# A decoder trunk on one core: the weights' low parts move from GpSimd to VectorE

## The reference

```python
for l in range(DEPTH):
    h = rms_norm(x, mix_norm[l])
    z = h @ w_in[l]
    c_q, c_kv, k_r, hq, hf, hi, hg, guv, gates = split_sizes(z, IN_SIZES)
    y_a = mla(c_q, c_kv, k_r, ..., cos, sin) @ w_branch_a[l]
    y_b = hgrn2(hq, hf, hi, hg, lower_bounds[l], hg_head_norm[l]) @ w_branch_b[l]
    y_c = gmlp(guv, gm_ln_g[l], gm_ln_b[l], gm_w_s[l], gm_b_s[l]) @ w_branch_c[l]
    g_a, g_b, g_c = jnp.split(jax.nn.sigmoid(gates), 3, axis=-1)
    x = x + (g_a * y_a + g_b * y_b + g_c * y_c) @ w_mix_out[l]
    h = rms_norm(x, xa_norm[l])
    m = rms_norm(mem, mem_norm[l])
    x = x + cross_attn(h, m, xa_w_q[l], xa_w_kv[l], xa_w_o[l])
    h = rms_norm(x, ffn_norm[l])
    gt, up = jnp.split(h @ ffn_w_in[l], 2, axis=-1)
    x = x + (jax.nn.silu(gt) * up) @ ffn_w_out[l]
return rms_norm(x, final_norm)
```

## Time and profile before

| | |
|---|---|
| median of 3 runs | 2306.24 us |
| lowest, highest | 2301.65, 2307.18 us |
| span of the profiled execution, first to last instruction | 2302.0 us |
| time of that execution beside its span | not given apart; the median of the runs is 4.2 us above the span |
| granted TensorE clock, mean over the span | 0.990 |
| GpSimd: busy, instructions | 899.5 us, 418 |
| ScalarE: busy, instructions | 1001.0 us, 1455 |

### The profile page before, as it was taken

One profiled execution on the slowest core, in us unless ns is written; L12 is line 12 of the kernel. 1 busy time (PEld: TensorE's weight loads), 2 busy tenths in 40 slices (PEclk: granted clock), 3 DMA queues, 4 the chain that ended last, 5 costly groups with the idle time before them and its releaser, 6 DMA issues.

```text
span 2302.0 us, 31660 instructions
## 1 busy us (share of the span) xinstructions
PE 2206.0 (96%) x10429; PEld 1788.9 (78%) x10429; DVE 1252.5 (54%) x1695; ACT 1001.0 (43%) x1455; POOL 899.5 (39%) x418
## 2 busy tenths in 40 slices
PE   6999999999999999999999999999999999999998
PEld 5787777667877888888878877776687878888886
DVE  6757666665654544441267566765556446444312
ACT  5665545444444333232356655454453444332223
POOL 4332333234544344444443332222354434444442
PEclk8999999999999999999999999999999999999999
DMA  5222221223333333333342222122343323333331
GB/s 160 72 67 65 65 57 47 56 77 112 113 95 101 90 92 101 92 98 92 95 121 65 69 60 65 39 62 52 102 115 92 109 84 95 98 101 92 94 100 63
DMA packets 368096, 197.10 MB, mean 86 GB/s; under 512 B 24268, under 2 KB 361528, under 8 KB 367928
## 3 DMA queue, kind: packets, MB, share of 16 engines
q1 hardware_dynamic: 362008, 185.68, 28.9%
q10 hardware_dynamic: 5920, 9.31, 1.3%
HBM read 191.68 MB, written 2.10 MB: 84 GB/s over the span
## 4 chain that ended last, share of the span: by engine, by line
PE 80%; DVE 10%; issue 5%; ACT 3%; DMA 1%; ACTq 0%; DVEq 0%; POOL 0%; SPq 0%; POOLq 0%
PE PS L573 23%; PE PS L575 23%; PE PS L574 23%; PE PS L792 2%; PE PS L733 1%; PE PS L815 1%; DVE rstd L1532 1%; DVE xqL L1306 1%; DVE mp L1612 1%; DMA spare<-mq 1%; DVE dec L1496 1%; DVE sqs L1274 1%; PE PS L630 1%; PE PS L632 1%; PE PS L631 1%
## 5 line engine op out<-in xcount | busy, mean ns | idle before, releaser
L513 POOL TENSOR_TENSOR wL<-raw,wH 128x1024 fp32r<-128x1024 f32 (+4 forms) x406 | 890.3, 2195 | 1361.0 <-ACT wH L936 1360.5
L936 ACT ACTIVATE wH<-raw 128x1024 fp32r<-128x1024 f32 (+4 forms) x406 | 384.1, 947 | 982.2 <-PE PS L575 892.1
L573 PE MATMUL PS<-hH,wH 128*128 128x512 f32 x1696 | 675.2, 398 | 16.0 <-ACT wH L936 11.0
L575 PE MATMUL PS<-hH,wL 128*128 128x512 f32 x1696 | 663.0, 391 | 0.0
L574 PE MATMUL PS<-hL,wH 128*128 128x512 f32 x1696 | 663.0, 391 | 0.0
L573 PEld LDWEIGHTS PS<-hH,wH 128*128 128x128 f32 x1696 | 319.9, 189 | 87.7 <-issue 13.1
L574 PEld LDWEIGHTS PS<-hL,wH 128*128 128x128 f32 x1696 | 320.1, 189 | 68.3 <-issue 3.6
L575 PEld LDWEIGHTS PS<-hH,wL 128*128 128x128 f32 x1696 | 319.5, 188 | 68.3
L1284 DVE TENSOR_TENSOR xT<-xT,PS 128x512 f32<-128x512 f32 x48 | 33.0, 688 | 264.3 <-PE PS L575 264.3
L1301 DVE TENSOR_TENSOR fm<-PS,rh 128x512 f32<-128x512 f32 x44 | 30.4, 692 | 201.1 <-PE PS L575 201.1
L575 PE MATMUL PS<-fH,wL 128*128 128x512 f32 x352 | 136.9, 389 | 0.0
(11 more groups left out here) (340 smaller groups left out, 3427.9 us busy)
## 6 DMA issues: line engine op xcount, KB each, us to landing
raw<-in_w_in SPq DMA_DIRECT2D x106, 512.0 KB, 3.9
raw<-in_ffn_w_in SPq DMA_DIRECT2D x88, 512.0 KB, 3.8
raw<-in_xa_w_kv SPq DMA_DIRECT2D x32, 512.0 KB, 3.8
raw<-in_ffn_w_out SPq DMA_DIRECT2D x32, 512.0 KB, 3.9
raw<-in_w_mix_out SPq DMA_DIRECT2D x16, 512.0 KB, 4.0
raw<-in_xa_w_q SPq DMA_DIRECT2D x16, 512.0 KB, 3.9
raw<-in_xa_w_o SPq DMA_DIRECT2D x16, 512.0 KB, 4.0
raw<-in_ffn_w_out SPq DMA_DIRECT2D x16, 384.0 KB, 3.4
```

The costliest lines, as they stand in the source:

```text
L513: nc.gpsimd.tensor_tensor(wL[:, s, 0:w], raw[:, r, 0:w], wH[:, s, 0:w].bitcast(F32), ALU.subtract).then_inc(*did("gpsimd", "lo", n))
L573: nc.tensor.matmul(o, w0, xh(k0 + k), start=(first and k == 0), stop=False)
L575: ins = nc.tensor.matmul(o, w1, xh(k0 + k), start=False, stop=(last and k == kts - 1))
L936: nc.scalar.activation(wH[:, PLACE[n] % NS, 0:w], raw[:, PLACE[n] % NR, 0:w], ACT.Copy).then_inc(*did("scalar", "hi", n))
```

## The change

The loop over the units leaves GpSimd. VectorE makes the same subtractions: those of units 0 to 3 at the head of the layer's loop, and that of each unit in freed(n) at the end of its step for unit n, after that step's evictions and low parts. What counts a "lo" is now VectorE's semaphore, for which SyncE and TensorE wait.

```diff
@@ GpSimd
             layers("gpsimd")
-            with pool.Fori(0, L) as l:
-                for n, (name, j) in enumerate(UNITS):
-                    kt, m = shape_of(name, j)
-                    w = kt * m
-
-                    pool.wait_ge(*after(l, "hi", n))
-                    s, r = PLACE[n] % NS, PLACE[n] % NR
-                    nc.gpsimd.tensor_tensor(wL[:, s, 0:w], raw[:, r, 0:w], wH[:, s, 0:w].bitcast(F32), ALU.subtract).then_inc(*did("gpsimd", "lo", n))
             ends("gpsimd")
@@ VectorE
+            def weight_low(l, n):
+
+                kt, m = shape_of(*UNITS[n])
+                w, s, r = kt * m, PLACE[n] % NS, PLACE[n] % NR
+                dve.wait_ge(*after(l, "hi", n))
+                V.tensor_tensor(wL[:, s, 0:w], raw[:, r, 0:w], wH[:, s, 0:w].bitcast(F32), ALU.subtract).then_inc(*did("vector", "lo", n))
+
             with dve.Fori(0, L) as l:
 
                 dve.wait_ge(*earlier(l, "vector"))
+                for n in range(NS):
+                    weight_low(l, n)
                 low_x(l, "mix", KT - 1, "mix_last", col("mix_norm", KT - 1))
...
                                 low(l, fL[:, k, :], fm[:, k % 2, :], fH[:, k, :], ("f_hi", k), "f_lo", k)
+                    if kind == "u":
+                        for q in freed(UNIT_AT[step[1:]]):
+                            weight_low(l, q)
```

## The result

The changed kernel takes 2275.3 us (median of 4 runs, 2272.7 to 2276.5) against 2306.7 for the kernel before (4 runs, three of them those of the table ahead): a ratio of 0.9865, with a 95% interval of 0.9851 to 0.9879. The forecast was 2276.

A forecast was written before the change was run, and what follows sets the result against it. TensorE was taken as the bound, its idleness partly from VectorE instructions stretched by GpSimd's reads; -24.2 waits, -10.2 clock, -6.0 hgrn, +3.4 MLA start, +1.3 start and gMLP, +5.2 boundary gave -30.5: 2276 us, range 2264 to 2299.

The forecast's parts named there:

- sqs: Sum of squares before the norm: VectorE's backlog after the mix units vanishes, and with it 8.2 us of TensorE's waits.
- MLA's heads: MLA heads 2 to 8, both layers: -14.4 us, mq's waits 7.6 and clock 6.8.
- Rival 4: Slower: the length is the instruction's own; at 2.4 us per 1024-column subtraction on VectorE, 2338 us; chance 0.09.
- rival 3: No difference: removed waits fall through to others just behind, such as DMA or ScalarE's table loads; 2308 us; chance 0.07.
- xqL with its clock: Cross-attention, both layers: -11.8 us, all 8.4 of the waits for xqL and 3.4 of clock.
- head 0: First hgrn head: VectorE waits for a high part behind ScalarE's logarithms; TensorE waits 1.7 us more per layer.
- 10.2 us if the gaps go: Lowered clock after gaps before MLA heads and the norm, 3.4 and 1.7 us a layer, regained; lower bound 0.
- Start and gMLP: First weights ready 1.1 us earlier, gMLP +1.2 us a layer from nine added subtractions: +1.3 us in all.
- The start of MLA: Before the first MLA head, three subtractions and a ScalarE wait lengthen TensorE's 0.86 us wait by 1.7: +3.4 in two layers.
- The layer boundary: Second layer's start: VectorE reaches the first subtractions only after fo's last eviction, TensorE idles some 3.5 us; +5.2 once.
- rival 2: VectorE waits in line for ScalarE's high parts, delaying evictions; hgrn and clock gains are lost: 2292 us; chance 0.22.
- The count of 54: Subtractions of 1024 columns taken to stand on VectorE's path, some 27 a layer in gMLP, hgrn heads and before MLA.

The follow-up runs named there:

- the 68 us: Changed kernel plus a useless GpSimd subtraction of the raw buffer behind each VectorE one: 2343.0 us, 68 us above the changed kernel.
- the run with the two repairs: Changed kernel with units 0 to 3 of each layer back on GpSimd and late subtractions at the three hgrn head boundaries: 2252.3 us.
- that run's 5 us: Changed kernel plus, per unit, a GpSimd subtraction of 16 columns and a memset of the rest: 2280.6 us, 5 us above the changed kernel.

## Why the prediction was right, and where it was not

**The diagnosis.** That the length of fL was a wait for GpSimd's reading is shown from both sides: 683 ns when it is taken away, 2788 when it is given back in the feed-forward. For sqs it is a row of 2.88 us beside the one GpSimd instruction there, for hlf eight of 2.38 beside GpSimd's reading and none beside its writing. xqL and mq have the one side only: short without GpSimd. That reading costs time at the level of the kernel is shown by the 68 us, though at other places than before; that its removal is what gained in MLA's heads, mix and cross-attention is shown by the kernel that takes GpSimd's reading away there alone and keeps the gain. Rival 4 (the length is the instruction's) fell with 1219 ns, rival 3 (no difference) with the result. Its page rule, the Trainium skill's "Perfetto Trace Analysis", section "Optimizing Scalar/DVE Operations" (an offload between GpSimd and VectorE might not help, since they share a read port), agrees with the first half of a layer, where the run with the early units on GpSimd comes out even (395.1 us, and 393.1 on VectorE); for the kernel as a whole the measured 1.35% decides against it.

**The terms that held.** sqs (-8.5 for -8.2), xqL with its clock (-14.3 for -11.8), MLA's heads (-13.4 for -14.4), feed-forward nothing. In hgrn2 the idleness fell by 8.2 us where 6.0 were forecast, and longer matmuls took 3.8 of it. In head 0 the forecast was that VectorE would wait for a high part behind ScalarE's logarithms and TensorE, which waited 0.20 us there, 1.7 more:

```profile
144.62 1.23 DVE L1330 TENSOR_TENSOR wL<-raw,wH 128x1024 fp32r<-128x1024 f32 x1 [1.77 <-ACT wH L928]
```

```profile
160.56 0.79 PE L687 MATMUL PS<-ident,hlf 128*128 128x128 f32 x4 [1.74 <-DVE hlf L1477]
```

It waited 1.74, so 1.5 more.

**The clock.** "10.2 us if the gaps go" counted only the stretches of the earlier trace rows. They did come back: in MLA's heads TensorE's busy time fell by 3.42 and in cross-attention by 2.8 a layer. But the granted clock fell elsewhere, on the way into MLA (+3.05), after the last head (+1.68), in hgrn2 (+2.85 and +0.97), at the layer boundary (+1.97), and the total of busy time is +0.3 where the clock terms on record make -9.7 (10.2, less 0.5 at the boundary). This is the step that failed: the clock term had regained stretches in it and, but for 0.5 us, no new ones. I asked which lowered stretches would go and never where new ones might come, though the sum itself had put longer waits into head 0, the start of MLA and the layer boundary. How far the new waits drew them the kept traces show in part. Into MLA the clock never fell where TensorE idled under 1 us (6 stretches, two of them before) and fell in 13 of the 20 where it idled 1.7 us or more. But after the last head the idleness is 2.06 us in every kernel, before and after alike, and the clock fell there in 13 of 26: those 3.4 us of the two layers are no work of a new wait. A sum can give such a term only as a chance.

**Start and gMLP.** +1.3 was forecast, -4.8 came. All but 0.4 of it is layer 1. "Nine subtractions add 11.3" on a VectorE that is busy 41.49 of 50 us is true of its load and not of the path: TensorE's idleness in gMLP of layer 1 fell from 2.62 to 1.98 us and its clock rose from 0.98 to 1.00. The term for the first weights held: idleness in the first stretch fell by 1.19 us, for 1.1. In sum: clock was 10.0 us worse than forecast and idleness 6.9 better (-27.7 for -20.8), which leaves 3.1 on the span; the median hides these too, since it lies 0.7 us above the span now, not 4.2. Of the 4.2, 1.8 is what each run has above its span, and 2.4 is which execution the profiler happened to take. So that the forecast came within 1 us is in good part luck: two errors of opposite sign, and this one besides.

**The start of MLA.** The wait did grow by 0.9 a layer (forecast 1.7); the rest is clock, above.

**The layer boundary.** +5.2 forecast, +6.6 measured, of a different make:

```profile
1141.64 0.74 DVE L1256 SCALAR_TENSOR_TENSOR hL<-xT,cur,hH 128x512 fp32r<-128x512 f32 x1
1142.30 0.68 DVE L1266 TENSOR_TENSOR sqs<-sqs,sq 128x512 f32<-128x512 f32 x1
1144.86 3.50 DVE L1330 TENSOR_TENSOR wL<-raw,wH 128x1024 fp32r<-128x1024 f32 x3 [1.88 <-issue]
1146.32 0.79 PE L565 MATMUL PS<-hH,wH 128*128 128x512 f32 x1 [5.33 <-DVE wL L1330]
...
1150.34 1.06 ACT L928 ACTIVATE wH<-raw 128x1024 fp32r<-128x1024 f32 x1 [12.33 <-DMA raw<-in_w_in]
...
1151.43 1.23 DVE L1330 TENSOR_TENSOR wL<-raw,wH 128x1024 fp32r<-128x1024 f32 x1 [3.07 <-ACT wH L928]
1152.58 0.74 DVE L1256 SCALAR_TENSOR_TENSOR hL<-xT,cur,hH 128x512 fp32r<-128x512 f32 x1
```

TensorE idled 5.33 us and not 3.5: between the last sum of fo and the first subtraction VectorE has 1.88 us in which it waits for nothing that the profile shows, the turn of its loop, and the sum had none. The fourth unit's late transfer and high part, and hL behind them, came as forecast; yet hL cost no wait of its own, since the first unit's products, at 0.79 us each where the kernel runs 0.39, lasted long enough.

**The markers.** The prediction called itself wrong if VectorE showed long idleness ahead of wL that ScalarE ends. It shows 172.4 us of that, in 135 waits, and rival 2 still did not come: some 120 of it falls in the feed-forward, where VectorE has nothing late behind it. The marker should have named TensorE. A second marker, TensorE waiting for wL elsewhere than at the layer's start, is met by the 1.9 us ahead of MLA's scores in the list above; but those matmuls read no weight, and the wL is what VectorE makes just behind the mq that they need. And not every sqs is below 1 us: the four at the start are not. The estimate of VectorE's busy time, at most 1527 us, gave back only fL and sqs; 1352.5 came.

**The count of 54** was a single number for something that is not linear: 38 by the run without subtractions (46.1/1.22), 66 by the doubled ones.

## What to carry to other kernels

Where one shape has several lengths on VectorE, look for GpSimd reading at the same time; but price the cure by where TensorE waits, since here 92 us of stretch in fL were worth nothing and 28 in xqL stood behind 8.4 us of TensorE's waits. When work is moved onto an engine, the place in its stream is worth as much as the move: the same three subtractions a few instructions later, in a wait that was there already, gave another 20 us on top of the 31. And a prediction that counts regained clock has to ask where clock may be lost anew, and to give it as a range: here the same waits lost it in about half of the cases.

## What the runs showed of the hardware

- The same pause drew a lowered clock in one execution and not in another. Before the last head's product with mpt TensorE waits some 2.06 us in every kernel (the 4.1 us in two waits for mpt); in the run with the two repairs the eight matmuls then took 2.37 us, in the run with the subtraction behind q 0 moved 3.92:

```profile
505.04 2.37 PE L829 MATMUL PS<-mpt,mv 128*64 128x512 f32 x8 [2.06 <-ACT mpt L1188]
```

```profile
506.79 3.92 PE L830 MATMUL PS<-mpt,mv 128*64 128x512 f32 x8 [2.06 <-ACT mpt L1189]
```

  The stretch around them was 60.22 us at a granted clock of 1.00 in the one and 61.84 at 0.97 in the other. Of the 26 such stretches in the 13 kept traces 13 are of the one kind and 13 of the other. What decides it no run here shows. Such steps of 1.6 us fit the spread between runs, whose times go with their granted clocks; that they make it is not shown.
- More idleness mostly went with more busy time: TensorE's busy sum was 2192.5 us without subtractions (37 us idle), 2206.3 in the changed kernel (68), 2230.8 with doubled ones (129), for the same 10429 matmuls. It is no law: the kernel before has 96 us idle and 2206.0.
- GpSimd's memset beside VectorE left two-operand instructions alone, but a few one-operand ones became longer: eight of `red<-red` 32x512 took 5.1 us together instead of 3.4, two of `ang<-ang` 2.4 instead of 1.0. That may be a part of that run's 5 us.
